# A four-stage decoder trunk on one core: LayerNorm weight moved to VectorE, an early root for the retention heads, sample state transfers on SyncE's queue, the first gated score level in quarters

## The reference

```
layer 0 mixer: z = x @ w_in                       # 3600 columns
   gated linear attention, 4 heads (q_g, k_g, v_g, gate r_g)
   retention, 4 heads               (q_r, k_r, v_r, gate g_r)
   o_g = rms_head_norm(o_g) * silu(r_g);  o_r = group_norm(o_r) * silu(g_r)
   y   = concat(o_g, o_r) @ w_out;  new states of both kinds, prompt and samples
layer 1 mixer: gated short convolution
after each mixer:  x = LN(ALPHA * x + y) ; then a gated ConvFFN, and again
                   x = LN(ALPHA * x + ffn) ;   LN(x) = (x - mean) / sqrt(var + eps) * g + b
```

## Time and profile before

| | us |
|---|---|
| median of 3 runs (lowest, highest) | 1330.37 (1330.33, 1330.70) |
| the profiled execution, its own time | 1330.02 |
| its span | 1328.2 |
| TensorE busy | 1267.6 (95%) |
| VectorE busy | 689.8 (52%) |
| ScalarE busy | 487.5 (37%) |
| GpSimd busy | 107.4 (8%) |

### The profile page before, as it was taken

The page is one execution under the profiler, slowest core; times in us unless marked ns, Lnnn a source line. Parts: engine busy times, 40 slices in busy tenths (PEclk is TensorE's granted clock), DMA queues, the critical chain, the costliest instruction groups (busy, mean ns, idle before and its releaser), DMA issues.

```text
span 1328.2 us, 23793 instructions
## 1 busy us (share of the span) xinstructions
PE 1267.6 (95%) x10717; PEld 1243.6 (94%) x10717; DVE 689.8 (52%) x1033; ACT 487.5 (37%) x703; POOL 107.4 (8%) x109
## 2 busy tenths in 40 slices
PE   6999989789899999999998999999899999999995
PEld 6999988689899999999998999998899999999995
DVE  4567964446465555562225244456466556552225
ACT  3444231535544343441215433225544343432111
POOL 3000000003300000000004200004200000000003
PEclk9999999889999999999999999999999999999998
DMA  8232134212122222222222222222222222223411
GB/s 266 66 97 84 58 113 126 79 64 96 65 96 95 83 82 93 96 88 88 95 88 96 64 96 96 96 65 96 64 96 96 96 96 95 81 74 105 131 63 65
DMA packets 123593, 122.47 MB, mean 92 GB/s; under 512 B 2481, under 2 KB 121164, under 8 KB 123476
## 3 DMA queue, kind: packets, MB, share of 16 engines
q1 hardware_dynamic: 112916, 115.32, 27.0%
q10 hardware_dynamic: 10432, 5.24, 1.4%
q0 software_dynamic: 144, 0.39, 0.1%
HBM read 114.79 MB, written 6.55 MB: 91 GB/s over the span
## 4 chain that ended last, share of the span: by engine, by line
PE 87%; ACT 4%; DVE 4%; POOL 3%; issue 1%; DMA 1%; POOLq 0%; ACTq 0%; SPq 0%
PE ps L354 26%; PE ps L356 25%; PE ps L355 25%; PE ps L373 3%; POOL ln_s L1009 2%; PE ps L377 2%; ACT x_hi L1239 1%; ACT x L1240 1%; POOL x_lo L1013 1%; ACT w_hi L336 1%; PE ps L571 1%; PE ps L502 1%; PE ps L733 0%; ACT o_tok_r L1160 0%; DMA x_tok<-in_x_sample 0%
## 5 line engine op out<-in xcount | busy, mean ns | idle before, releaser
L354 PE MATMUL ps<-x_hi,w_hi 128*128 128x256 f32 (+1 forms) x2048 | 584.3, 285 | 0.7 <-ACT a_samp L1047 0.7
L356 PE MATMUL ps<-x_hi,w_lo 128*128 128x256 f32 (+1 forms) x2048 | 579.5, 283 | 0.0
L355 PE MATMUL ps<-x_lo,w_hi 128*128 128x256 f32 (+1 forms) x2048 | 577.5, 282 | 0.0
L354 PEld LDWEIGHTS ps<-x_hi,w_hi 128*128 128x128 f32 x2048 | 386.8, 189 | 6.4 <-issue 5.1
L355 PEld LDWEIGHTS ps<-x_lo,w_hi 128*128 128x128 f32 x2048 | 387.8, 189 | 0.1
L356 PEld LDWEIGHTS ps<-x_hi,w_lo 128*128 128x128 f32 x2048 | 386.9, 189 | 0.0
L343 DVE TENSOR_TENSOR w_lo<-w_raw,w_hi 128x2048 fp32r<-128x2048 f32 (+2 forms) x103 | 235.6, 2289 | 167.5 <-ACT w_hi L336 167.2
L354 PE MATMUL ps<-h_hi,w_hi 128*128 128x264 f32 (+1 forms) x896 | 254.9, 284 | 0.1
L355 PE MATMUL ps<-h_lo,w_hi 128*128 128x264 f32 (+1 forms) x896 | 252.7, 282 | 0.0
L356 PE MATMUL ps<-h_hi,w_lo 128*128 128x264 f32 (+1 forms) x896 | 252.7, 282 | 0.0
L336 ACT ACTIVATE w_hi<-w_raw 128x2048 fp32r<-128x2048 f32 (+2 forms) x103 | 192.6, 1870 | 160.4 <-DMA w_raw<-in_w_ffn_out 140.6
(11 more groups left out here) (249 smaller groups left out, 1118.4 us busy)
## 6 DMA issues: line engine op xcount, KB each, us to landing
w_raw<-in_w_ffn_in SPq DMA_DIRECT2D x44, 1024.0 KB, 4.9
w_raw<-in_w_ffn_out SPq DMA_DIRECT2D x16, 1024.0 KB, 5.1
w_raw<-in_w_mix_in SPq DMA_DIRECT2D x14, 1024.0 KB, 5.1
w_raw<-in_w_sc_in SPq DMA_DIRECT2D x12, 1024.0 KB, 5.0
w_raw<-in_w_ffn_out SPq DMA_DIRECT2D x8, 768.0 KB, 4.5
w_raw<-in_w_mix_out SPq DMA_DIRECT2D x4, 1024.0 KB, 5.2
w_raw<-in_w_sc_out SPq DMA_DIRECT2D x4, 1024.0 KB, 5.2
x_tok<-in_x_prompt SPq DMA_DIRECT2D x2, 1024.0 KB, 7.4
```

Source lines behind the costliest of these rows:

```text
L354: e.matmul(out, wh, xh[:, k, lo:hi], start=(first and i == 0), stop=False)
L355: e.matmul(out, wh, xl[:, k, lo:hi], start=False, stop=False)
L356: mm = e.matmul(out, wl, xh[:, k, lo:hi], start=False, stop=(last and i == len(ks) - 1))
```

## The change

Four parts.

1. **Score levels.** Level 0 computes two blocks of 64 x 64 tokens for each chunk and head instead of one of 128 x 128 (on TensorE the same form as the levels 2 to 7), and VectorE merges each level but 1 and 2 with two predicated copies, each on 64 partitions and half of the columns, instead of one on 128 partitions.
2. **Heads.** The prompt's 16 retention groups get a root of their own after T18 (`hn_root(1)`) and are normalised after T19; the samples' group has its root after T20 (`hn_root(2)`) and is normalised ahead of the copy of T21. `ret_outer((2, 3))` moves into T19, and each `heads_turn` one tile forward, so that behind T23 there is none. VectorE makes `ret_keys` ahead of the sums and statistics of the gated heads.
3. **Sample states.** The stores and loads move to SyncE's queue, behind the weight loads 12 to 15.
4. **LayerNorm.** Of the squares GpSimd adds tmp[0..3]; VectorE adds tmp[4..5] and tmp[6..7] in one instruction and then the two sums. `ln_var` and `ln_spread` come some k-steps earlier. In the first half all eight tiles are scaled in one go. In the second half VectorE multiplies by weight and 1/root in one instruction, ScalarE only adds the bias into x_hi, GpSimd makes the even tiles (bias into x32, then x_lo), VectorE the odd ones (`split_odd`), whose bias GpSimd adds to x32 afterwards.

The diff at its core:

```diff
             for u in range(8, U_OUT[0] + 8):
                 load_unit(e, u)
+                if u == 12:
+                    gla_samples_store()
+                elif u == 13:
+                    ret_samples_load((0, 1))
+                elif u == 14:
+                    ret_samples_load((2, 3))
+                elif u == 15:
+                    ret_samples_store()
...
-                        rows = C if n == 0 else C // 2
-                        for row in ((0,) if n < 2 else (0, C // 2)):
+                        rows = C // 2
+                        for row in ((0,) if n == 1 else (0, C // 2)):
...
             def ret_samples_out():
 
-                e.wait_ge(sem("samp_made"), 2 + RH)
+                e.wait_ge(sem("head_read_g"), 2)
...
-                [lambda: ret_outer((0, 1))], [lambda: ret_outer((2, 3))], [lambda: heads_turn((0, 1))], [lambda: heads_turn((2, 3))],
-                [lambda: heads_turn((4, 5))], [lambda: heads_turn((6, 7))]]
+                [lambda: ret_outer((0, 1))], [lambda: heads_turn((0, 1))], [lambda: heads_turn((2, 3))],
+                [lambda: heads_turn((4, 5))], [lambda: heads_turn((6, 7))], []]
             inside = [[] for _ in range(15)] + [
-                [gla_samples_out], [lambda: samples_turn(1)], [lambda: ret_chunks((0, 1))], [], [], [ret_samples_out], [], [], []]
+                [gla_samples_out], [lambda: samples_turn(1)], [lambda: ret_chunks((0, 1))], [], [lambda: ret_outer((2, 3))],
+                [ret_samples_out], [], [], []]
...
-                    at, piece = {(1, 0, 1): (4, lambda: ln_mean(n, 0)), (2, 0, 1): (6, lambda: ln_var(n, 0)),
-                                 (2, 1, 1): (4, lambda: ln_spread(n, 0))}.get((j, f, h), (None, None))
+                    at, piece = {(1, 0, 1): (4, lambda: ln_mean(n, 0)), (2, 0, 1): (1, lambda: ln_var(n, 0)),
+                                 (2, 1, 1): (0, lambda: ln_spread(n, 0))}.get((j, f, h), (None, None))
...
-                    if k == 3:
+                    if k == 2:
...
-                        if (f, k) == (1, 5):
+                        if (f, k) == (1, 2):
...
-                    for t in range(1, KD - 2):
+                    for t in range(1, KD // 2):
                         e.wait_ge(sem("ln_squared"), KD * (2 * n + h) + t + 1)
                         if t > 1:
-                            e.wait_ge(sem("ln_added"), (KD - 3) * (2 * n + h) + t - 1)
+                            e.wait_ge(sem("ln_added"), (KD // 2 - 1) * (2 * n + h) + t - 1)
                         e.tensor_tensor(ln_s2[:, lo:hi], tmp[:, 0, lo:hi] if t == 1 else ln_s2[:, lo:hi], tmp[:, t, lo:hi], ALU.add
                                         ).then_inc(sem("ln_added"), 1)
-                    for t in range(KD):
-                        e.wait_ge(sem("x_new"), KD * (2 * n + h) + t + 1)
+                    for t in range(0, KD, 1 + h):
+                        if h == 0:
+                            e.wait_ge(sem("x_new_0"), KD * n + t + 1)
+                        else:
+                            e.wait_ge(sem("x_hi_made"), KD + KD * (2 * n + h) + t + 1)
+                            e.tensor_tensor(x32[:, t, lo:hi], x32[:, t, lo:hi], bias_of(n, t).broadcast_to([P, hi - lo]), ALU.add
+                                            ).then_inc(sem("x_new"), 1)
+                            e.wait_ge(sem("x_new"), 5 * n + t // 2 + 1)
                         e.tensor_tensor(x_lo[:, t, lo:hi], x32[:, t, lo:hi], x_hi[:, t, lo:hi].bitcast(F32), ALU.subtract
                                         ).then_inc(sem("x_made"), 1)
+                lo, hi = HALVES[1]
+                e.wait_ge(sem("x_made_odd"), KD // 2 * (n + 1))
+                for t in range(1, KD, 2):
+                    ins = e.tensor_tensor(x32[:, t, lo:hi], x32[:, t, lo:hi], bias_of(n, t).broadcast_to([P, hi - lo]), ALU.add)
+                ins.then_inc(sem("x_new"), 1)
...
-                     [ret_values], [lambda: ret_outputs((2, 3)), lambda: ret_samples_load((2, 3))],
-                     [], [lambda: ret_samples_store((0, 1))], [lambda: ret_samples_store((2, 3))],
-                     [lambda: hn_root(1), lambda: head_hi((0, 1))], [hn_norm, lambda: head_hi((2, 3))], [lambda: head_out((4, 5))]]
+                     [gla_decays, gla_values], [gla_keys, lambda: samples_copy(0)], [], [], [gla_outputs], [], [], [],
+                     [ret_values], [lambda: ret_outputs((2, 3))],
+                     [lambda: hn_root(1)], [lambda: hn_norm(range(16))],
+                     [lambda: head_hi((0, 1)), lambda: hn_root(2)],
+                     [lambda: head_hi((2, 3)), lambda: head_out((4, 5))], [lambda: head_out((6, 7)), lambda: head_hi((4, 5))], []]
             inside = [[] for _ in range(16)] + [
-                [lambda: samples_copy(1), lambda: hn_root(0)], [lambda: ret_samples_load((0, 1)), lambda: ret_outputs((0, 1))],
-                [], [], [], [], [], []]
+                [lambda: samples_copy(1)], [lambda: hn_root(0), lambda: ret_outputs((0, 1))],
+                [], [], [], [lambda: hn_norm((16,))], [], []]
...
+                    if h:
+                        e.activation(x_hi[:, t, lo:hi], x32[:, t, lo:hi], ACT.Identity, bias=bias_of(n, t)).then_inc(sem("x_hi_made"), 1)
+                        continue
+                    e.activation(x_hi[:, t, lo:hi], x32[:, t, lo:hi], ACT.Identity, bias=bias_of(n, t), scale=gain_of(n, t)
+                                 ).then_inc(sem("x_hi_made"), 1)
+                    e.activation(x32[:, t, lo:hi], x32[:, t, lo:hi], ACT.Identity, bias=bias_of(n, t), scale=gain_of(n, t)
+                                 ).then_inc(sem("x_new_0"), 1)
...
-                e.copy_predicated(sc[:, :, :].rearrange("p h (c t) -> p (h c) t", t=C), bc(masks[:, (n - 1) % (LEVELS + 1), :], 1, GH * NC),
-                                  ps_t[:, 4 * 512:8 * 512].rearrange("p (m t) -> p m t", t=C)).then_inc(sem("level_added"), 1)
+                for lo in (0, C // 2):
+                    hi = lo + C // 2
+                    ins = e.copy_predicated(sc[lo:hi, :, :].rearrange("p h (c t) -> p (h c) t", t=C)[:, :, lo:hi],
+                                            bc(masks[lo:hi, (n - 1) % (LEVELS + 1), lo:hi], 1, GH * NC),
+                                            ps_t[lo:hi, 4 * 512:8 * 512].rearrange("p (m t) -> p m t", t=C)[:, :, lo:hi])
+                ins.then_inc(sem("level_added"), 1)
...
-                [lambda: rotate(k_r, (2, 3), 7)], [ret_queries, gla_sample_states], [ret_scores, lambda: head_parts(0, range(NC))],
-                [lambda: samples_masked(0), lambda: samples_summed(0), lambda: head_stats(0), ret_keys], [],
-                [lambda: ret_states((0, 1)), lambda: head_inverse(0)], [lambda: ret_states((2, 3)), lambda: head_parts(1, range(NC))],
-                [lambda: ret_sample_states((0, 1))], [lambda: ret_sample_states((2, 3)), lambda: samples_masked(1), lambda: samples_summed(1),
-                lambda: head_stats(1)], [lambda: head_gated((0, 1)), lambda: head_inverse(1)], [lambda: head_gated((2, 3)), lambda: head_lo((0, 1))],
-                [lambda: head_lo((2, 3))]]
+                [lambda: rotate(k_r, (2, 3), 7)], [ret_queries, gla_sample_states], [ret_scores],
+                [lambda: samples_masked(0), ret_keys, lambda: samples_summed(0)], [lambda: link(head_parts(0, range(NC))), lambda: head_stats(0, range(17))],
+                [lambda: ret_states((0, 1)), gla_inverse],
+                [lambda: ret_states((2, 3)), lambda: link(head_parts(1, range(NC))), lambda: head_stats(1, range(16)),
+                 lambda: ret_sample_states((0, 1))],
+                [lambda: ret_inverse(2, slice(0, 16)), lambda: ret_sample_states((2, 3))],
+                [lambda: head_gated((0, 1)), lambda: samples_masked(1), lambda: samples_summed(1), lambda: head_stats(1, (16,))],
+                [lambda: head_gated((2, 3)), lambda: ret_inverse(3, slice(16, 17)), lambda: head_lo((0, 1))],
+                [lambda: head_lo((2, 3)), lambda: head_gated((4, 5))], []]
...
-                e.tensor_tensor(tmp[:, 6, lo:hi], tmp[:, 6, lo:hi], tmp[:, 7, lo:hi], ALU.add).then_inc(sem("ln_squares"), 1)
+                link(e.tensor_tensor(tmp[:, 4:6, lo:hi], tmp[:, 4:6, lo:hi], tmp[:, 6:8, lo:hi], ALU.add))
+                e.tensor_tensor(tmp[:, 4, lo:hi], tmp[:, 4, lo:hi], tmp[:, 5, lo:hi], ALU.add).then_inc(sem("ln_squares"), 1)
...
+                    if h == 0:
+                        ins = e.tensor_tensor(x32[:, t, lo:hi], x32[:, t, lo:hi], bank(6 + h, P, 0, hi - lo), ALU.mult)
+                    else:
+                        ins = e.scalar_tensor_tensor(x32[:, t, lo:hi], x32[:, t, lo:hi], gain_of(n, t), bank(6 + h, P, 0, hi - lo),
+                                                     ALU.mult, ALU.mult)
+                    ins.then_inc(sem("ln_scaled"), 1)
+
+            def split_odd(n, tiles):
+
+                lo, hi = HALVES[1]
+                for t in tiles:
```

(19 more changed lines are left out.)

123 lines of the change are left out of this document (60 added, 63 removed).

## The result

The changed kernel takes 1292.12 us in the median (1291.7 to 1292.41, 4 runs), the kernel before 1330.35 (1330.05 to 1330.7, 4 runs): 0.9711 of it, 95% interval [0.9696, 0.9726], 38.2 us less. The forecast was 1300 us with a range from 1293 to 1309; the time lies 0.9 us under the range. The profiled execution took 1291.7 us.

The account below looks back on a forecast made before the run. TensorE, busy for 1267.6 us, was taken to bound the kernel. Terms −0.9 + 0.2 − 2.4 − 16.9 − 10.2 = −30.2 us from 1330.02 gave 1300 us, range 1293 to 1309.

Parts of the forecast that it names:

- Score levels: Gated scores: level 0 takes 0.9 us less on TensorE; VectorE's split copies add 0.2 us of wait at level 6.
- Keys, and the wait that stays: Retention keys: the 1.2 us waits at L660 and L596 go, −2.4 us; v_tok's 1.2 us at L679 stays.
- Heads: Retention heads: waits of 9.0 and 3.6 us go, 0.7 is added, half clock gives 5.0: −16.9 us.
- both half-clock stretches: TensorE at half clock from 253.6 to 263.85 and 270.7 to 277.5 us; expected to go, −2.4 − 2.6 us.
- State transfers: Sample-state loads and stores on SyncE's queue: states are ready before the next weight load is due, so no time gained.
- Norms: Three norms: 10.2 of 18.7 us of waits stay, 6.0 of it for x_lo; with the clock's 1.7 us, −10.2 us.
- The rest of the norms: Norms' waits for w_lo, about 1.2 us each, plus 0.6 us for norm 1's sum: 4.2 us stay.
- The third stretch of half clock: TensorE at half clock from 731.5 to 734.9 us, inside norm 1; should go with that norm's waits, 1.7 us.
- (c): Norms better: x_lo pairs never wait and w_lo is covered; up to 10 us more, 1290 to 1295; chance 0.08.
- (a): Heads: the samples' chain replaces the old wait, TensorE waits 3 to 4 us; 1306 to 1307; chance 0.15.
- (d): SyncE's queue: a state store blocks a weight load and TensorE waits for weights; slower, above 1333; chance 0.02.
- (b): Norms give little: split_odd also stops GpSimd's pairs, so 2 us gained instead of 10; 1308; chance 0.12.

Follow-up runs that it names:

- e3: Kernel before with the score-level part alone (level 0 in quarters, predicated copy in two): 1329.73 us, ratio 0.9994 [0.9985, 1.0003].
- e2: Kernel before with only the second and third parts (head norms and piece order, sample-state transfers on SyncE's queue): 1310.01 us, ratio 0.9850.
- e9: Kernel after without ScalarE's second wait on the same gla_out count ahead of T16's copy: 1290.82 us, ratio 0.9709.
- e4: Kernel after with the samples' state loads and stores given back to ScalarE's queue: 1292.00 us, ratio 0.9707.
- e5: Kernel before with VectorE's w_lo of unit m+2 waiting until GpSimd has made all eight second-half x_lo: 1327.26 us, ratio 0.9969.
- e13: Kernel after with VectorE's w_lo of unit m+2 put ahead of its last two split_odd: 1293.61 us.
- e1: Kernel before with the fourth part (norms) alone: 1314.37 us, ratio 0.9878.

## Why the prediction came out 8 us too high

- **Score levels: right.** Level 0 now takes 1.1 us (63.7 to 64.8 us). VectorE's two copies take 2.66 us together against 2.50, so 0.16 us and not 0.35 of surcharge, and level 6 waits 0.15 us where 0.2 was forecast. e3 gives −0.7, the sum on record, with an interval that takes in no change.
- **Keys, and the wait that stays: right.** L660 and L596 have no successors in the list, v_tok's 1.2 us is there.
- **Heads: right, and as tight as said.** The chain of the samples' group was added up to 7.1 us against 7.3; it took 6.9 (copy of T20 at 232.65, o_samp normalised at 239.51 us) and TensorE came at 240.20:

```profile
232.65 0.61 ACT L1113 ACTIVATE g_r<-ps 128x520 f32<-128x520 f32 x1 [2.62 <-PE ps L356]
...
236.12 1.28 ACT L1189 ACT_TABLE_LOAD   x1
237.42 0.30 ACT L1189 ACTIVATE hn_inv<-hn_stats,eps 128x1 f32<-128x1 f32 x1
239.01 0.50 ACT L1196 ACTIVATE o_samp<-o_samp,hn_shift,hn_inv 128x128 f32<-128x128 f32 x1 [1.30 <-DVE hn_shift L1643]
```

The new wait of 0.7 us ahead of the projection is there with its number, both half-clock stretches are gone, and e2 measures −20.4 for keys and heads where the sum had 2.4 + 16.9 = 19.3. By the trace 20.7 us are gained ahead of the norms, where levels, keys and heads together had 20.0. Between the end of the work before the table load (236.10) and the root behind it (237.42) lie 1.32 us. The Trainium skill ("ScalarE: Activation LUTs", section "What ACT_TABLE_LOAD costs") adds a drain of the same size; no row here shows one, and e9's gain fits a load of 1.28 us.
- **State transfers: right.** e4.
- **Norms: the step that failed.** The forecast kept 6.0 us of x_lo's waits, 2.0 for each norm: "in the middle of GpSimd's third pair, and holds it for 2.3 us or so, of which 0.5 are covered". The hold is real (2.68 us, e5, e13). Its place was off: GpSimd's pair takes 1.5 us (0.62 + 0.83), not 1.7, and w_lo meets the fourth pair. And its cover was off, which weighs more: e13 puts w_lo into the third pair and it costs 0.5 us a norm (1.5 us in all), because the third x_lo ends at 322.65 us undisturbed while TensorE wants it at 324.23, 1.6 us later. The forecast compared GpSimd's rate with TensorE's for two tiles (1.7 against 2.2 us) and never summed the lead that this builds up over pairs. What stays is 0.3 us a norm for the first tile, forecast at 0.2: 5.1 us too few were taken off.
- **The rest of the norms, mis-sized.** w_lo and the sums leave 4.6 us where 4.2 were forecast, and the mean 0.1 more than before. Against that, all waits were summed from TensorE's matmuls; by the weight loads the norms' waits fell by 14.7 us (from 11.5 + 8.0 + 3.2 + 0.7 = 23.4 to 1.5 + 3.1 + 3.2 + 0.9 = 8.7; x_lo, sum of squares, w_lo, mean), by the matmuls by 13.1. So 5.1 − 0.4 − 0.1 + 1.6 = 6.2 us of the 8 are in this part. The two marks in the norms say that it is more: 17.7 us were gained between them where 10.2 were forecast, 7.5 of the 8. The 1.3 us over waits and clock stand in neither list of waits and stay open. Ahead of the norms only 0.7 us was forecast too little, so most of what e2's median has over its terms is not in the trace.
- **The third stretch of half clock** went, as forecast. That norm 1's waits alone were its cause is not shown: in e1 they were gone but for one of 2.19 us, which came with later weights, and the stretch stood behind it.
- **Rivals.** (c) is what happened in its first half, x_lo's pairs waiting no longer but for the first, and its range of 1290 to 1295 us holds the measured time; w_lo was not covered. It stood at 0.08. (a) and (d) did not come about: no wait for o_samp, none for the states or for weights near them. (b) rested on the `split_odd` stopping GpSimd for 0.4 to 0.5 us each. The Trainium skill ("SBUF — State Buffer", section "SBUF: two separate sides") lets a VectorE instruction with two SBUF inputs and a GpSimd one exclude each other for their length. The trace agrees for w_lo; beside `split_odd` GpSimd's instructions read 0.82 to 0.88 us against 0.75 alone, so that four of them cost it well under 1 us a norm, in a place with cover.

## What to carry to other kernels

When an instruction of one engine holds up a row of instructions on another, follow the lead of that row over its consumer tile by tile, up to the tile that is held; comparing rates and taking one tile's slack as the cover priced the hold at 1.8 us here, where 0.5 was measured. Sum TensorE's waits from the weight loads' rows, not only from the matmuls', when many short ones are at stake. Before a conversion is moved forward, look when its operand lands: the wait may move to the DMA and hit all that is queued behind it. And a second wait on a count that has already been waited for was not free where a table load stood behind it: without it the load ran 2.4 us earlier in e9.
